# Splitting fp32 weights: the high part on GpSimd in one copy, every low part on VectorE

## The chip, the core and the metric

The kernel runs on one core of a Trainium2 chip, as one launch. The metric is device time in microseconds (us), from the start to the end of the execution. TensorE multiplies, VectorE (DVE) and ScalarE (ACT) do the elementwise work, GpSimd (POOL) helps with it, and SyncE (SP) issues most of the transfers from HBM. SBUF is the memory on the core that all of them read.

## The reference, cut to what matters

Two residual stacks of two layers run on 256 latent tokens (and, in the first stack, on 256 context tokens too), all in float32 with 1024 channels.

```
for l in range(2):                               # first stack
    context:  mixer (l = 0) or its memory only (l = 1), then FFN
    latent:   x = post(x, mixer(modulate(x)), gate);  x = post(x, ffn(modulate(x)), gate)
mixer = w_out( g_att * (attention @ w_att_o) + g_gla * (gated linear attention @ w_gla_o)
             + g_conv * (depthwise conv of 31 taps, layernorm, silu) @ w_conv_o )
for l in range(2):                               # second stack
    x += mix4(rmsnorm(x) @ w_in) @ w_o ;  x += (silu(h @ w_gate) * (h @ w_up)) @ w_down
```

Nearly all weights are used once per pass, as dense products of 256 tokens with matrices of 1024 or 2816 columns (the FFN is `silu(h @ gate) * (h @ up)` times `down`).

## The kernel before, in words

**The split.** A float32 product is made of three cheaper ones: a weight tile w is split into w_hi (w rounded to fp32r) and w_lo = w - w_hi, the activations into h_hi and h_lo, and TensorE adds w_hi h_hi, w_hi h_lo and w_lo h_hi (`dense`, L484 to L486; `dense_together`, L497 on; `token_major`, L512 on). A tile is 128 x 128 and meets 256 tokens, so one tile costs three matmuls.

**The stream.** All these tiles lie in HBM in the order of their use, as 723 loads of 8 tiles (128 x 1024 floats, 512 KB each). Three slots in SBUF hold a load's raw form, its high and its low part (`w_raw`, `w_hi`, `w_lo`, L211 to L213). For every load four things happen in turn. SP issues the transfer when the low part of the load three places earlier is made (L434). The high part is made when the transfer has landed and when TensorE has begun the load two places earlier, so that it is done with the old tiles of the slot (semaphore `w_used`). The low part is made from `w_raw` and `w_hi`. TensorE waits for the low part at a load's first tile (L456), and increments `w_used` with the load's first matmul.

**Who splits, before.** ACT makes the high part in two pieces of 512 columns (`split_to`, L1062 to L1074). ACT is in order: it evacuates each finished PSUM bank (`arrived` and `moved`), and `split_to` is called at those places, two to three loads ahead of TensorE. The low part is made by one of two engines, by a static plan. POOL makes it in the FFNs in one piece of 1024 columns, and in four pieces of 256 in the first loads of each pass, in the pass that only makes the context's memory and in the mixers of the second stack (`low_parts`, L1032 to L1055). DVE makes it in the three whole mixers of the first stack (`lows`, L1617 to L1624, called from `evac`), in one instruction of 1024 columns. `mixer_at` and `ffn_at` record at which loads these stretches begin. No low part is made by DVE in an FFN or in the second stack.

**What DVE does else.** In the mixers of the first stack it computes the depthwise convolution as a chain of multiply-adds of 256 columns (`convolve`, L1750 to L1765, 30 taps for 8 chunks), which is cut into 24 pieces of 10 instructions and placed between the other steps, many of them in the attention (L2125). It computes the scans and the differences of the gated linear attention (`gla`), the softmax's maxima and normalisation (`attention`), and all low parts of activations (`both_parts`, L1699, `low_part`, L1658). In an FFN it multiplies gate and up (L1739), splits the product (L1700, L1701) and adds the residual (L1718, L1723). The FFN is a loop of two turns, 33 loads each (`feed_forward`), so the counts of semaphores in it depend on the turn (`Place.value`, L377, with the increments of one turn in `PER_HALF`, L54).

**How far ahead.** `evac` lets DVE make all low parts up to one or two loads past the one that holds the chunk it is about to wait for; `tile_at` (L474) says where each chunk ends in the stream.

The functions with their lines:

Of the kernel before, what the change touches and what calls it, by code (L numbers as in the profile page):

```python
# [28 lines left out]
P = 128  # L29
D = 1024  # L30
KC = D // P
# [22 lines left out]
PER_HALF = {"lin_done": 2 * HALF + KC, "lin_evac": 2 * HALF + KC, "lo_ready": 3 * HALF, "hi_ready": 6 * HALF,  # L54
# [4 lines left out]
PIECES = 4  # L59
# [138 lines left out]
def program(nc, stream, first_in, ada_in, xt_in, cvec_in, vec1_in, vec2_in, glr_in, a2_in, const1_in, const2_in, small2_in, mask_in, out):  # L198
# [5 lines left out]
    with ExitStack() as ctx:  # L204
# [236 lines left out]
        ffn_at = []  # L441
        mixer_at = []
# [3 lines left out]
        def _(pe):  # L446
# [25 lines left out]
            def done(mm):  # L472
                mm.then_inc(sems["lin_done"], 1)
                if at.turn is None:  # L474
                    tile_at[n.at("lin_done")] = max(at.tile, tile_at.get(n.at("lin_done") - 1, 0))
# [209 lines left out]
            def feed_forward():  # L685
                h0 = n.at("h_ready") - KC
                ffn_at.append(at.tile // TILES)
# [110 lines left out]
            for turn, (l, s) in enumerate(PASSES):  # L798
# [35 lines left out]
                    mixer_at.append(at.tile // TILES)  # L834
# [195 lines left out]
        @block.gpsimd  # L1030
        def _(pool):
            def low_parts(first, last, pieces):  # L1032

                def one(load, slot):
                    for q in range(pieces):
                        if q * 2 % pieces == 0:
                            pool.wait_ge(sems["hi_ready"], load * 2 + (1 if q * 2 < pieces and pieces > 1 else 2))
                        part = slice(q * TILES * P // pieces, (q + 1) * TILES * P // pieces)
                        ins = pool.tensor_tensor(w_lo[:, slot, part], w_raw[:, slot, part], w_hi[:, slot, part].bitcast(F32), ALU.subtract)  # L1039
                    ins.then_inc(sems["lo_ready"], 1)  # L1040
                if last - first >= SLOTS:
                    with pool.Fori(0, (last - first) // SLOTS) as i:
                        for s in range(SLOTS):
                            one(i * SLOTS + (first + s), (first + s) % SLOTS)
                for load in range(last - (last - first) % SLOTS, last):
                    one(load, load % SLOTS)
            assert len(ffn_at) == 5 and len(mixer_at) == 3
            low_parts(0, SLOTS, PIECES)
            for k, load in enumerate(ffn_at):
                if k < len(mixer_at):  # L1050

                    pool.wait_ge(sems["lo_ready"], load)
                low_parts(load, load + 6 * HALF, 1)
                following = [x + SLOTS if x in mixer_at else x for x in sorted(mixer_at + ffn_at) + [LOADS] if x > load][0]
                low_parts(load + 6 * HALF, following, PIECES)  # L1055

        @block.scalar
        def _(act):
# [3 lines left out]
            def split_to(load):  # L1062

                while at.split < load:
                    m = at.split
                    at.split += 1
                    slot, turn = m % SLOTS, m // SLOTS
                    add = 16 * (turn + 1)
                    act.wait_ge(landed[slot], add if at.turn is None else at.turn * (16 * HALF) + add)
                    if m - SLOTS >= at.tile_done // TILES:  # L1070

                        act.wait_ge(sems["w_used"], at.value("w_used", m - SLOTS + 1))
                    for part in (slice(0, TILES * P // 2), slice(TILES * P // 2, TILES * P)):
                        act.activation(w_hi[:, slot, part], w_raw[:, slot, part], ACT.Copy).then_inc(sems["hi_ready"], 1)  # L1074

            def arrived(tiles=KC):

                at.tile += tiles
                if tiles:
                    split_to((at.tile - 1) // TILES + SLOTS)  # L1080
# [312 lines left out]
            def first_modulated():  # L1393
# [6 lines left out]
                split_to(SLOTS)  # L1400
# [201 lines left out]
            split_to(LOADS)  # L1602
# [3 lines left out]
        def _(dve):  # L1606
# [107 lines left out]
            def residual(x, alpha, means, early=None):  # L1714

                for c in range(KC):
                    dve.wait_ge(sems["lin_evac"], evac() if at.turn is None else at.up("lin_evac"))
# [14 lines left out]
            def feed_forward(x, scaled):  # L1732
                a, _ = CONST1["alpha"]
                with dve.Fori(0, 2) as i:
                    at.enter(i, dve_step=2 * HALF + (KC - 2) * scaled)
                    for c in range(HALF):
                        dve.wait_ge(sems["lin_evac"], at.up("lin_evac", 2))
# [6 lines left out]
                    at.leave()  # L1744
                dve.wait_ge(sems["r_ready"], at.now("r_ready"))
# [205 lines left out]
            def gla_memory(l, s):  # L1951
                n.up("lin_evac", 4 + len(MEMORY_UNITS[:2]))
                scans()
                for u in MEMORY_UNITS[2:]:
# [504 lines left out]
```

## Time and profile before

| | |
|---|---|
| median of 3 runs (lowest to highest) | 3263.15 us (3260.86 to 3266.92) |
| the profiled execution's own time | 3261.29 us |
| its span in the profile | 3259.5 us |
| mean granted TensorE clock | 0.94 |
| PE, PEld busy | 2966.9, 2806.7 us |
| DVE busy | 2195.1 us |
| ACT busy | 1517.4 us |
| POOL busy | 1057.0 us |

The table is one execution. Busy time is the time in which an engine had an instruction in work; it includes time in which an instruction had started and could not go on. PE is the matmul side of TensorE, PEld its weight loads. The span is cut below into stretches by their place in the kernel: the first mixer of the first stack runs from about 60 to 600 us, its FFN to about 840 us; the two other whole mixers begin near 860 and 1760 us, the pass that makes only the context's memory lies between 1660 and 1760 us, and the second stack begins near 2550 us.

### The profile page before, as it was taken

To read this page: it belongs to the slowest core of one execution; us is meant where nothing else is said; L and a number is where in the kernel's file an instruction comes from. 1 tells how busy PE (TensorE), PEld (TensorE's weight loads), DVE (VectorE), ACT (ScalarE), POOL (GpSimd) and SP (SyncE) were. 2 spreads that over 40 slices of the span, in tenths; PEclk is the share of its full clock that TensorE was granted. 3 is DMA by queue.
4 is the path that set the end of the run, shared out by engine and by line. 5 is a ranking of instruction groups with operands and counts; after the bars stand their busy time and mean duration, and the time that the engine had idled before them with its cause. 6 is when DMAs were issued, how large, how long until landed. Compare 5 with 4: busy or idle time off the path is not lost.

```text
span 3259.5 us, 57687 instructions
## 1 busy us (share of the span) xinstructions
PE 2966.9 (91%) x21812; PEld 2806.7 (86%) x21812; DVE 2195.1 (67%) x3303; ACT 1517.4 (47%) x3128; POOL 1057.0 (32%) x646
## 2 busy tenths in 40 slices
PE   8999979899889988989988899889899989998998
PEld 7998868899889878889978898679899869996998
DVE  6774787576778577775745775877666557646665
ACT  3544335444554424444454544235444454555554
POOL 1000000188200000037851000000388627873787
PEclk7999979899999988999989999889899989999999
DMA  6443324355444323435533443224455314541454
GB/s 240 150 154 111 123 90 146 105 183 175 135 155 137 103 97 102 145 109 171 181 98 110 150 152 101 77 73 154 153 175 180 105 53 161 172 155 56 144 176 164
DMA packets 120727, 441.85 MB, mean 136 GB/s; under 512 B 13456, under 2 KB 15504, under 8 KB 119872
## 3 DMA queue, kind: packets, MB, share of 16 engines
q1 hardware_dynamic: 108704, 393.35, 36.7%
q10 hardware_dynamic: 11808, 45.42, 4.1%
q8 instruction: 161, 2.64, 0.3%
q14 instruction: 54, 0.44, 0.0%
HBM read 437.67 MB, written 1.05 MB: 135 GB/s over the span
## 4 chain that ended last, share of the span: by engine, by line
PE 42%; issue 20%; DVE 17%; POOL 15%; ACT 5%; POOLq 0%; DMA 0%; SPq 0%; DVEq 0%; ACTq 0%
POOL w_lo L1039 15%; PE lin L484 9%; PE lin L486 9%; PE lin L485 9%; DVE arena L1763 7%; DVE w_lo L1622 3%; PE lin L534 3%; PE aux L734 2%; ACT w_hi L1074 1%; PE aux L597 1%; PE aux L622 1%; PE aux L588 1%; DVE small L1777 1%; ACT arena L1234 1%; DVE s_lo L1701 1%
## 5 line engine op out<-in xcount | busy, mean ns | idle before, releaser
L1039 POOL TENSOR_TENSOR w_lo<-w_raw,w_hi 128x1024 fp32r<-128x1024 f32 (+1 forms) x642 | 1056.8, 1666 | 2196.0 <-ACT w_hi L1074 2195.5
L484 PE MATMUL lin<-h_hi,w_hi 128*128 128x256 f32 x3584 | 1039.8, 290 | 47.0 <-DVE w_lo L1622 31.5
L485 PE MATMUL lin<-h_lo,w_hi 128*128 128x256 f32 x3584 | 1024.2, 286 | 0.0
L486 PE MATMUL lin<-h_hi,w_lo 128*128 128x256 f32 x3584 | 1023.5, 286 | 0.0
L1074 ACT ACTIVATE w_hi<-w_raw 128x512 fp32r<-128x512 f32 x1446 | 827.4, 623 | 119.2 <-PE lin L484 108.7
L484 PEld LDWEIGHTS lin<-h_hi,w_hi 128*128 128x128 f32 x3584 | 699.9, 195 | 59.4 <-issue 29.6
L485 PEld LDWEIGHTS lin<-h_lo,w_hi 128*128 128x128 f32 x3584 | 699.5, 195 | 0.4
L486 PEld LDWEIGHTS lin<-h_hi,w_lo 128*128 128x128 f32 x3584 | 698.0, 195 | 0.0
L1622 DVE TENSOR_TENSOR w_lo<-w_raw,w_hi 128x1024 fp32r<-128x1024 f32 x315 | 381.2, 1219 | 213.0 <-ACT w_hi L1074 211.7
L484 PE MATMUL lin<-s_hi,w_hi 128*128 128x256 f32 x1392 | 408.4, 293 | 16.6 <-DVE s_lo L1701 7.4
L485 PE MATMUL lin<-s_lo,w_hi 128*128 128x256 f32 x1392 | 400.9, 288 | 0.0
L486 PE MATMUL lin<-s_hi,w_lo 128*128 128x256 f32 x1392 | 400.6, 288 | 0.0
L484 PEld LDWEIGHTS lin<-s_hi,w_hi 128*128 128x128 f32 x1392 | 274.3, 197 | 24.7 <-issue 14.4
L1763 DVE SCALAR_TENSOR_TENSOR arena<-arena,vec 128x256 f32<-128x256 f32 x720 | 290.5, 477 | 0.0
L485 PEld LDWEIGHTS lin<-s_lo,w_hi 128*128 128x128 f32 x1392 | 274.8, 197 | 1.1 <-issue 0.8
L486 PEld LDWEIGHTS lin<-s_hi,w_lo 128*128 128x128 f32 x1392 | 274.3, 197 | 0.0
L1739 DVE TENSOR_TENSOR y_buf<-gate_buf,y_buf 128x256 f32<-128x256 f32 x110 | 151.1, 1374 | 181.8 <-ACT y_buf L1207 181.8
L1701 DVE TENSOR_TENSOR s_lo<-y_buf,s_hi 128x256 fp32r<-128x256 f32 x110 | 224.2, 2038 | 3.8
L534 PEld LDWEIGHTS lin<-cvec,a_raw 128*128 128x128 f32 x1280 | 165.1, 207 | 11.9 <-DMA a_raw<-in_ada 9.3
L534 PE MATMUL lin<-cvec,a_raw 128*128 128x2 f32 x1280 | 162.1, 257 | 7.9 <-DMA a_raw<-in_ada 7.9
L1640 DVE RECIPROCAL rstd<-std 128x256 f32<-128x256 f32 (+1 forms) x34 | 59.5, 1749 | 150.8 <-ACT std L1103 150.7
L1718 DVE SCALAR_TENSOR_TENSOR X<-X,gate_buf 128x256 f32<-128x256 f32 x72 | 75.5, 1049 | 125.0 <-ACT gate_buf L1215 67.1
(265 smaller groups left out, 4272.6 us busy)
## 6 DMA issues: line engine op xcount, KB each, us to landing
w_raw<-in_stream SPq DMA_DIRECT2D x723, 512.0 KB, 3.4
a_raw<-in_ada ACTq DMA_DIRECT2D x80, 512.0 KB, 3.4
arena<-in_first SPq DMA_DIRECT2D x2, 2048.0 KB, 19.6
X<-in_tokens SPq DMA_DIRECT2D x2, 1024.0 KB, 14.7
s_f<-in_ada SPq DMA_DIRECT2D x4, 512.0 KB, 10.5
arena<-in_ada SPq DMA_DIRECT2D x4, 512.0 KB, 17.3
arena<-in_const ACTq DMA_DIRECT2D x1, 1856.0 KB, 8.6
arena<-in_small ACTq DMA_DIRECT2D x1, 1536.0 KB, 12.7
```

The source lines that it names most:

```text
L484: used(pe.matmul(o, whi, hi[:, k, :], start=k == 0, stop=False), first)
L485: pe.matmul(o, whi, lo[:, k, :], start=False, stop=False)
L486: mm = pe.matmul(o, wlo, hi[:, k, :], start=False, stop=k == kcs - 1)
L534: mm = pe.matmul(o[:, 0:2], w[:, k, :], cvec[:, k, :], start=k == 0, stop=k == KC - 1)
L734: mm = pe.matmul(pair[kt][:, h * P:(h + 1) * P], part, part, start=True, stop=True)
L1039: ins = pool.tensor_tensor(w_lo[:, slot, part], w_raw[:, slot, part], w_hi[:, slot, part].bitcast(F32), ALU.subtract)
L1074: act.activation(w_hi[:, slot, part], w_raw[:, slot, part], ACT.Copy).then_inc(sems["hi_ready"], 1)
L1622: dve.tensor_tensor(w_lo[:, m % SLOTS, :], w_raw[:, m % SLOTS, :], w_hi[:, m % SLOTS, :].bitcast(F32), ALU.subtract).then_inc(sems["lo_rea ...
L1701: dve.tensor_tensor(lo, y, hi.bitcast(F32), ALU.subtract).then_inc(sems[name], 1)
L1718: dve.scalar_tensor_tensor(x[:, c, :], x[:, c, :], alpha, gate_buf[:, c % 2, :], ALU.mult, ALU.add).then_inc(sems["r_ready"], 1)
L1739: step(dve.tensor_tensor(y, gate_buf[:, c % 2, :], y, ALU.mult))
L1763: dve.scalar_tensor_tensor(CV[:, c, :], YP[:, c, tap:tap + S], v1(l, "conv_w", c * TAPS + tap), CV[:, c, :], ALU.mult, ALU.add).then_inc(s ...
```

## The change

The high part of every load is made by POOL in one `tensor_copy` of 1024 columns, as soon as the load has landed and `w_used` allows. The low part of every load is made by DVE (`lows`), in the FFN loops, the memory pass and the second stack too. ACT has neither. The static plan (`mixer_at`, `ffn_at`), `low_parts` and `split_to` are gone. `hi_ready` counts one per load where it counted two.

```
         def _(pool):
+            def high_part(s):
+                pool.tensor_copy(w_hi[:, s, :], w_raw[:, s, :]).then_inc(sems["hi_ready"], 1)
+            for load in range(USED + 2):
+                pool.wait_ge(landed[load % SLOTS], 16 * (load // SLOTS + 1))
+                if load >= SLOTS:
+                    pool.wait_ge(sems["w_used"], load + 1 - SLOTS)
+                high_part(load % SLOTS)
...
         def _(act):
-            def split_to(load):
...
             def moved(ins):
                 ins.then_inc(sems["lin_evac"], 1)
-                split_to(at.tile // TILES + SLOTS)
...
         def _(dve):
-            low_next = [0, 0]
+            low_next = [0]
             def lows(load):
-                first, last = low_next
-                for m in range(first, min(load, last)):
-                    dve.wait_ge(sems["hi_ready"], 2 * m + 2)
+                for m in range(low_next[0], load):
+                    dve.wait_ge(sems["hi_ready"], at.value("hi_ready", m + 1))
                     dve.tensor_tensor(w_lo[:, m % SLOTS, :], w_raw[:, m % SLOTS, :], w_hi[:, m % SLOTS, :].bitcast(F32), ALU.subtract
                                       ).then_inc(sems["lo_ready"], 1)
-                low_next[0] = max(first, min(load, last))
+                low_next[0] = max(low_next[0], load)
+            def lows_for(k):
+                lows(tile_at[n.at("lin_evac") + k] // TILES + SLOTS - 1)
             def evac(k=1):
-                c = n.up("lin_evac", k)
-                lows(tile_at[c] // TILES + SLOTS - 1)
-                return c
+                lows_for(k)
+                return at.up("lin_evac", k)
...
             def feed_forward(x, scaled):
                     for c in range(HALF):
-                        dve.wait_ge(sems["lin_evac"], at.up("lin_evac", 2))
+                        dve.wait_ge(sems["lin_evac"], evac(2))
```

`residual` in the FFN calls `evac` in the same way. In the memory pass the scans now carry the low parts between them. At the start two low parts stand before the first modulation (`lows(SLOTS - 1)`). In the second stack the waits for evacuations become `evac` calls, and `lows_for(8)` and `lows_for(2)` stand ahead of the first reciprocal and inside the pooling. POOL makes 720 high parts, so the last three loads of the padded stream are not split.

## Rows read from the trace of the kernel before

**Rows 1.** The page: busy time of each engine.

```profile
PE 2966.9 (91%) x21812; PEld 2806.7 (86%) x21812; DVE 2195.1 (67%) x3303; ACT 1517.4 (47%) x3128; POOL 1057.0 (32%) x646
```

**Rows 2.** Windows; the mixer's stretches and one in an FFN (busy us, count).

```profile
core 0: us, PE busy (x) PEld busy (x) DVE busy (x) ACT busy (x) POOL busy (x), PEclk, DMA share, GB/s
60.00:160.00 100.00, 93.08 (x743) 91.16 (x742) 74.29 (x129) 55.29 (x105) 0.00 (x0) 0.98 0.45 143
380.00:460.00 80.00, 64.00 (x444) 59.80 (x442) 75.84 (x185) 22.61 (x68) 0.00 (x0) 0.85 0.33 106
650.00:740.00 90.00, 88.24 (x734) 87.84 (x733) 63.79 (x47) 44.56 (x89) 76.87 (x32) 1.00 0.57 183
...
200.00:260.00 60.00, 59.87 (x506) 59.87 (x507) 52.22 (x74) 27.14 (x49) 0.00 (x0) 0.97 0.46 150
520.00:540.00 20.00, 13.44 (x96) 13.09 (x96) 19.35 (x43) 9.80 (x22) 0.00 (x0) 0.91 0.34 106
```

**Rows 3.** Windows of DVE's low parts alone (L1622), in mixer stretches of three passes.

```profile
60.00:160.00 100.00, 33.60 (x28) 0.98 0.45 143
380.00:460.00 80.00, 10.36 (x9) 0.85 0.33 106
...
200.00:260.00 60.00, 12.18 (x10) 0.97 0.46 150
520.00:540.00 20.00, 5.88 (x6) 0.91 0.34 106
...
1180.00:1260.00 80.00, 9.73 (x8) 0.88 0.33 111
...
2080.00:2190.00 110.00, 13.39 (x11) 0.84 0.23 72
```

**Rows 4.** The chain that ended last, by line, within 380 to 460 us.

```profile
by line: DVE arena L1763 67.3%; DVE w_lo L1622 10.0%; ACT arena L1234 6.2%; DVE small L1777 4.6%; DVE a_lo L1803 2.1%; DVE arena L1756 1.6%; ACT a_hi L1248 1.4%; DVE small L1782 1.3%; ACT w_hi L1074 1.3%; DVE M L1839 1.0%; DVE arena L1795 0
```

**Rows 5.** Groups of instructions with their shapes (busy us, mean ns, idle before).

```profile
L1039 POOL TENSOR_TENSOR w_lo<-w_raw,w_hi 128x1024 fp32r<-128x1024 f32 x330 | 808.1, 2453 | 1966.2 <-ACT w_hi L1074 1966.0
L1039 POOL TENSOR_TENSOR w_lo<-w_raw,w_hi 128x256 fp32r<-128x256 f32 x312 | 248.9, 834 | 229.8 <-ACT w_hi L1074 229.5
...
L1622 DVE TENSOR_TENSOR w_lo<-w_raw,w_hi 128x1024 fp32r<-128x1024 f32 x315 | 381.2, 1219 | 213.0 <-ACT w_hi L1074 211.7
L1763 DVE SCALAR_TENSOR_TENSOR arena<-arena,vec 128x256 f32<-128x256 f32 x720 | 290.5, 477 | 0.0
...
L1337 ACT ACTIVATE arena<-arena 128x1024 f32<-128x1024 f32 x48 | 50.6, 1053 | 22.7 <-DVE arena L1902 12.6 <-DVE arena L1897 6.6 <-issue 3.5
```

**Rows 6.** DVE's low parts of activations (L1701): duration min/median/max in ns.

```profile
L1701 DVE TENSOR_TENSOR s_lo<-y_buf,s_hi x110: 424/2511/2562, 652.3 to 3210.9; 128x256 fp32r<-128x256 f32 x110
L1701 DVE TENSOR_TENSOR s_lo<-s_f,s_hi x24: 424/426/427, 332.2 to 2031.0; 128x256 fp32r<-128x256 f32 x24
```

**Rows 7.** Timeline in an FFN, DVE and POOL from 699 us (start, us).

```profile
700.30 0.29 DVE L1700 CAST s_hi<-y_buf 128x256 fp32r<-128x256 f32 x1
700.63 2.51 DVE L1701 TENSOR_TENSOR s_lo<-y_buf,s_hi 128x256 fp32r<-128x256 f32 x1
...
700.38 2.48 POOL L1039 TENSOR_TENSOR w_lo<-w_raw,w_hi 128x1024 fp32r<-128x1024 f32 x1 [0.39 <-ACT w_hi L1074]
```

**Rows 8.** What PE waited for (us in total, times, longest).

```profile
PE lin L484 <- DVE w_lo L1622: 31.5, 19, 7.3
...
PE lin L484 <- POOL w_lo L1039: 12.6, 17, 1.0
PE lin L512 <- DVE w_lo L1622: 11.9, 9, 3.5
...
PE lin L512 <- POOL w_lo L1039: 9.0, 5, 4.0
...
PE lin L484 <- DVE s_lo L1701: 7.4, 10, 0.8
```

**Rows 9.** The page: the chain that ended last, by line.

```profile
POOL w_lo L1039 15%; PE lin L484 9%; PE lin L486 9%; PE lin L485 9%; DVE arena L1763 7%; DVE w_lo L1622 3%; PE lin L534 3%; PE aux L734 2%; ACT w_hi L1074 1%; PE aux L597 1%; PE aux L622 1%; PE aux L588 1%; DVE small L1777 1%; ACT arena L1234 1%; DVE s_lo L1701 1%
```

**Rows 10.** The second stack's pooling steps, DVE, from 2880 to 3030 us.

```profile
L2205 DVE TENSOR_TENSOR arena<-arena 128x542 f32<-128x542 f32 (+3 forms) x4 | 4.6, 1159 | 0.1
```

More of the change, by code:

```diff
@@ L52 @@
 NEG = -1e30
-PER_HALF = {"lin_done": 2 * HALF + KC, "lin_evac": 2 * HALF + KC, "lo_ready": 3 * HALF, "hi_ready": 6 * HALF,
+PER_HALF = {"lin_done": 2 * HALF + KC, "lin_evac": 2 * HALF + KC, "lo_ready": 3 * HALF, "hi_ready": 3 * HALF,
             "w_used": 3 * HALF, "s_ready": HALF, "r_ready": KC, "dve_step": 2 * HALF, "sum_ready": 1}
@@ L58 @@
 SLOTS = 3
-PIECES = 4
 ADA_CHUNKS = 6 * D // P
@@ L473, in done @@
                 mm.then_inc(sems["lin_done"], 1)
-                if at.turn is None:
-                    tile_at[n.at("lin_done")] = max(at.tile, tile_at.get(n.at("lin_done") - 1, 0))
+                tile_at[n.at("lin_done")] = max(at.tile, tile_at.get(n.at("lin_done") - 1, 0))
             def dense(hi, lo, ready=None, kcs=KC):
@@ L1031, in _ @@
         def _(pool):
[L1032 to L1055, printed above, removed]
+            def high_part(s):
[5 more added lines that the diff above has]
+                high_part(load % SLOTS)
         @block.scalar
@@ L1060, in _ @@
             n = at.n
-            def split_to(load):
[L1064 to L1074, printed above, removed]
             def arrived(tiles=KC):
                 at.tile += tiles
-                if tiles:
-                    split_to((at.tile - 1) // TILES + SLOTS)
                 act.wait_ge(sems["lin_done"], at.up("lin_done"))
@@ L1601, in _ @@
             at.tile_done = LOADS * TILES
-            split_to(LOADS)
         @block.vector
@@ L1716, in residual @@
                 for c in range(KC):
-                    dve.wait_ge(sems["lin_evac"], evac() if at.turn is None else at.up("lin_evac"))
+                    dve.wait_ge(sems["lin_evac"], evac())
                     dve.scalar_tensor_tensor(x[:, c, :], x[:, c, :], alpha, gate_buf[:, c % 2, :], ALU.mult, ALU.add
@@ L1744, in feed_forward @@
                     at.leave()
+                    assert low_next[0] == low_first + 3 * HALF
+                    low_next[0] += 3 * HALF
                 dve.wait_ge(sems["r_ready"], at.now("r_ready"))
@@ L1951, in gla_memory @@
             def gla_memory(l, s):
-                n.up("lin_evac", 4 + len(MEMORY_UNITS[:2]))
-                scans()
-                for u in MEMORY_UNITS[2:]:
-                    unit(l, u)
+                evac(4 + len(MEMORY_UNITS[:2]))
+                scans(lambda c: unit(l, MEMORY_UNITS[2:][c]))
                 dve.wait_ge(sems["x_ready"], n.at("x_ready"))
@@ L1997, in first_modulated @@
                 dve.tensor_tensor(wglr_lo[:, :], wglr[:, :], wglr_hi[:, :].bitcast(F32), ALU.subtract).then_inc(sems["glr_split"], 1)
+                lows(SLOTS - 1)
                 n.up("lin_evac", len(FIRST_UNITS) + len(FIRST_GROUPS))
@@ L2045, in _ @@
                         centre(before, early)
+                        evac(KVH + QT + 1)
                         scaled(early, lambda c: v1(pl, "ln2_g", c))
                         n.up("x_ready", KC)
-                        n.up("lin_evac", KVH + QT + 1)
                         inverse(aux[0], ROWS, name="row_ready")
+                        evac(2)
                         heads_normed(heads, {})
-                        n.up("lin_evac", 2)
                         gla_memory(l, s)
@@ L2057, in _ @@
                     y0, pieces = n.at("y_ready"), iter(range(CONV_PIECES))
-                    turns = [k for k, p in enumerate(PASSES) if whole(*p)]
-                    low_next[:] = mixer_at[turns.index(turn)] + SLOTS, ffn_at[turns.index(turn)]
                     for c in range(KC):
-                        if c == 0:
-                            dve.wait_ge(sems["lo_ready"], low_next[0])
                         dve.wait_ge(sems["lin_evac"], evac(2))
@@ L2189, in _ @@
                 step(dve.memset(w2["up"][:, :, 0:16], 0.0))
+                lows_for(8)
                 inverse(aux[0], slot=0)
@@ L2198, in _ @@
                 n.up("qk_normed")
-                dve.wait_ge(sems["lin_evac"], at.up("lin_evac", 9))
+                dve.wait_ge(sems["lin_evac"], evac(9))
                 prev, e = w2["up"], 16 + S
@@ L2206, in _ @@
                     prev = cur
+                lows_for(2)
                 ic = c2("inv_count").rearrange("p (c t) -> p c t", c=2)
@@ L2213, in _ @@
                 n.up("pooled_ready")
-                dve.wait_ge(sems["lin_evac"], at.up("lin_evac", 4))
+                dve.wait_ge(sems["lin_evac"], evac(4))
                 step(dve.tensor_tensor(w2["zp"][:, :, 2:], w2["gc"][:, :, :], w2["uc"][:, :, :], ALU.mult))
@@ L2225, in _ @@
                 cos, sin = c2("cos"), c2("sin")
-                dve.wait_ge(sems["lin_evac"], at.up("lin_evac", 3 + 2 * MH + 2))
+                dve.wait_ge(sems["lin_evac"], evac(3 + 2 * MH + 2))
                 dve.wait_ge(sems["rot_done"], at.up("rot_done"))
```

6 lines of the change are left out of this document (1 added, 5 removed).

## The prediction

> **What bounds the kernel now.** I began with the busy shares [rows 1]: PE is at 91% of the span, DVE at 67%, ACT at 47%, POOL at 32%. Those are averages over stages with different limits, so I cut the span into stretches [rows 2].
>
> In an FFN (650 to 740 us) PE is busy 88.24 of 90 us for 734 matmuls, 0.120 us each, or 24 x 0.120 = 2.89 us per load. There is nothing to win there but single waits. The chain puts 15% of the span on POOL's low parts [rows 9], but these lie beside a PE that is full; PE waited for them 12.6 + 9.0 us in the whole kernel [rows 8]. In the first stack's attention (380 to 460 us) it is the other way round: DVE 75.8 of 80 us, PE 64 with a granted clock of 0.85, and the chain in that stretch is DVE's convolution, 67.3%, and its low parts, 10.0% [rows 4]. Two shorter stretches are like it or near it: 520 to 540 us (DVE 19.35 of 20 us, PE 13.4) and 200 to 260 us (DVE 52.2 of 60, PE full) [rows 2]. So what the change is worth is read from DVE's time in the three whole mixers. In all of them POOL stands still today (0 us).
>
> **DVE and POOL get in each other's way.** This row decides the case. In FFNs the activation's low part, 256 columns, has a median of 2511 ns; the same instruction where POOL rests takes 426 ns [rows 6]. The timeline shows how: POOL starts at 700.38 and ends at 702.86, DVE's subtraction starts at 700.63 and ends at 703.14, 0.28 us after POOL [rows 7]. DVE waited for the whole of POOL's instruction, and only its fixed start of about 0.43 - 0.28 = 0.15 us was hidden. The cast at 700.30, with one input, ran its 0.29 us while POOL was starting. DVE's subtractions and convolution taps have two inputs in SBUF, and are of the kind that waited.
>
> **What moves.** ACT loses 1446 pieces, POOL its low parts. DVE gets 720 - 315 = 405 low parts more at 1.219 us [rows 5], 494 us of work. POOL gets 720 copies of 1024 columns. The queues of SP are not touched but for who releases them: the transfer of a load follows the low part, now always DVE's.
>
> **What one copy costs.** No row shows a one-input instruction of POOL. From below: a whole 1024-column instruction of ACT takes 1.053 us [rows 5], and I don't expect POOL to beat it. From above: the two-input one of the same size, 2.453 us. Between them, POOL's own slope: (2453 - 834) / 768 = 2.11 ns a column and 0.29 us fixed [rows 5]; if one input costs half of two, that is 0.29 + 1024 x 1.054 ns = 1.37 us, or 1.23 us if the fixed part halves too. I take 1.3 us, since the rows nearest to it are POOL's own. It adds 1.3 - 0.15 = 1.15 us to a DVE that has no idle time.
>
> The page "GPSIMD Engine Reference" of the Trainium skill (section 4.1, Engine selection) says that one-input work on GpSimd runs at roughly line rate, against about twice the time for two inputs. With one column per cycle of 1.2 GHz that would be an estimated 0.85 us and the fixed part, some 1.15 us, and the sum below would be about 22 us smaller. The page "SBUF — State Buffer" (section "SBUF: two separate sides") says that any GpSimd instruction that reads SBUF excludes DVE instructions with two SBUF inputs for its whole length. By that rule the copy blocks as the subtraction did; no row here shows it for a copy.
>
> **Losses, step by step.**
> - Attention: 9, 8 and 11 low parts fall in the DVE-bound stretches of the three passes [rows 3], so as many copies: 28 x 1.15 = 32 us. DVE is the chain there, so all of it counts.
> - Start of the mixer (60 to 160 us): DVE 74.29 + 28 x 1.15 = 106.5 us in 100 [rows 2, 3]: 6.5 us over, three passes, 20 us.
> - Linear attention (200 to 260 us): 52.22 + 10 x 1.15 = 63.7 in 60: 3.7 x 3 = 11 us.
> - Merge (520 to 540 us): 19.35 + 6 x 1.15 = 26.3 in 20; DVE has idle time right behind it, so I count half: 3 x 3 = 9 us.
> - Start of the kernel: two low parts ahead of the first modulation, 2 x 1.22 = 2.4 us.
> Together 74 us.
>
> **What is hidden.** FFN, two loads and one product: DVE 2 x 1.22 + 0.42 + 0.29 + 0.43 = 3.58 us, POOL 2 x 1.3 = 2.6 us. Even if they never overlap this is 6.18 us, less the hidden starts (five of 0.15) 5.4 us, against PE's 5.78 us. They are also out of step by nature: a copy follows the start of a load, the low part follows the copy. So the FFN costs nothing at 1.3 us; the cover is gone above about 1.5 us. Queued behind DVE's new waits for `hi_ready` are the FFN's products. The last low part asked for ahead of a product needs PE at the start of the load just before that product's end, 1.3 + 1.2 = 2.5 us of 2.89, so the product is not held. Second stack: the four pooling steps, 4.6 us [rows 10], stand between low parts, and two loads in hand cover 5.8 us. Zero, and if the cover breaks a few us per layer.
>
> **Gains.** POOL's low parts were late for PE by 12.6 + 9.0 us [rows 8], mostly where it takes four pieces of 0.834 us for a load that PE eats in 2.89 us; DVE's 1.22 us removes this. The FFN's last activation low part, blocked by POOL, cost 7.4 us at ten places, which goes too [rows 8]. ACT's high parts stand on the chain with 1% [rows 9], some 30 us; a copy of the same length takes their place, and only what came from ACT being busy elsewhere goes: 5 us. Together 34 us. What is late next is DVE's low part in the mixers (31.5 + 11.9 us of PE's waits already [rows 8]).
>
> **The sum** against the profiled execution: 3261.3 + 74 - 34 = 3301 us. That execution is 1.9 us below the median, so I say 3303 us, slower by 1.2%. A measurement of this kernel tells about 0.2% (6.5 us) from no change.
>
> **The rivals.**
> 1. *The copy is slow.* If POOL needs 1.7 us, a third of the way from my value to the upper bound, each copy costs 1.55: attention 43, mixer start (74.3 + 43.4 - 100) x 3 = 53, linear attention (52.2 + 15.5 - 60) x 3 = 23, merge 8.7 x 3 = 26, start 2; and the FFN is over by 3.58 + 3.4 - 0.75 - 5.78 = 0.45 us for each of 165 pairs, 74 us: 3261 + 221 - 34 = 3448 us. At the upper bound, 2.453 us, the same sum gives 267 us in the mixers and 1.95 x 165 = 322 in the FFNs: about 3816 us. For: POOL's other instruction is slow for its size. Against: it reads two inputs. Chance 0.19.
> 2. *The other side: ACT's queue was the hidden limit.* DVE stood idle 211.7 us before its low parts, waiting for ACT's high part [rows 5]. ACT is in order and makes it behind evacuations; POOL has nothing else and copies at once. If a good part of that idle time was ACT's and not PE's, DVE makes its low parts earlier and the collisions fall into time it had to spare. Then the stretches outside the attention cost nothing, attention pays at the lower bound, 28 x 0.9 = 25 us, and half of the 1% (33 us) that ACT's high parts have on the chain [rows 9] is gained: 3261 + 25 - 34 - 16 = 3236 us. It decides where ACT's lateness, not `w_used`, held the high part. Against: most of that idle lies where PE is full and where nobody is in a hurry. Chance 0.22.
> 3. *A wash.* The copy at the lower bound, 1.05 us: attention 25, linear attention 4, merge 7, start 2, mixer start none; 38 - 34 = +4 us: 3265 us. Chance 0.09.
> The forecast, a copy of 1.1 to 1.5 us that blocks DVE, keeps 0.5; its own range is 3275 to 3345 us.
>
> **Range and chances.** Down to 3230 us I take in rival 2, up to 3430 us the copies to about 1.65 us. Left out are the rest of rival 1 and what lies beyond rival 2, some 0.2. Faster 0.22, same 0.09, slower 0.69.
>
> **What would show it.** POOL's group has one form of 1024 columns with 1.2 to 1.4 us; 1.7 or more means rival 1. The convolution's taps, 477 ns before [rows 5], get a mean some 50 ns higher, with single ones near 1.6 us. PE's waits for DVE's low parts grow from 43 us, those for POOL vanish. The stretches of the three mixers become longer, attention most; the FFNs stay at 0.120 us per matmul. I am wrong if the taps keep their time, if the mixers become shorter, or if the FFN slows down while the copy is short.

## The result, and the profile after

| | before | after |
|---|---|---|
| median, measured together (lowest to highest) | 3265.03 us (3260.86 to 3267.48) | 3348.94 us (3346.33 to 3357.11) |
| the profiled execution's own time, span | 3261.29, 3259.5 us | 3351.34, 3349.5 us |

The ratio is 1.026 (95% interval 1.024 to 1.0285): slower by 2.6%, where 1.2% was forecast. The time lies inside the range (3230 to 3430 us) and the direction is the forecast's; the loss is twice the size. The page of after, its busy times and its chain by line (these answer to [rows 1] and [rows 9]):

```profile
PE 3008.8 (90%) x21812; PEld 2833.6 (85%) x21812; DVE 2440.8 (73%) x3708; ACT 768.4 (23%) x1682; POOL 894.0 (27%) x724
...
PE lin L480 14%; PE lin L481 13%; PE lin L482 13%; DVE arena L1727 8%; DVE w_lo L1580 6%; PE lin L530 3%; PE aux L729 3%; PE aux L593 2%; DVE rstd L1601 2%; POOL w_hi L1028 2%; DVE arena L1616 1%; PE aux L584 1%; ACT arena L1195 1%; DVE small L1741 1%; PE lin L493 1%
```

POOL's 15% of the chain are gone, and ACT's busy time is halved, yet DVE's convolution and low parts stand on the chain with 8% and 6% where they had 7% and 3%. PE's busy time grew by 41.9 us for the same 21812 matmuls, at a mean granted clock of 0.934 against 0.94: nearly half of the loss is not idle time in front of a matmul but PE taking longer over the same work. The groups of after with their shapes (busy us, mean ns, idle before; they answer to [rows 5]):

```profile
L1580 DVE TENSOR_TENSOR w_lo<-w_raw,w_hi 128x1024 fp32r<-128x1024 f32 x720 | 904.9, 1266 | 415.7 <-POOL w_hi L1028 409.4 <-DVE mod L1794 0.7
L1028 POOL CAST w_hi<-w_raw 128x1024 fp32r<-128x1024 f32 x720 | 893.8, 1243 | 2439.6 <-PE lin L480 1932.6 <-PE lin L493 314.3 <-DMA w_raw<-in_stream 127.3
...
L1727 DVE SCALAR_TENSOR_TENSOR arena<-arena,vec 128x256 f32<-128x256 f32 x720 | 334.2, 535 | 0.0
...
L1662 DVE TENSOR_TENSOR s_lo<-y_buf,s_hi 128x256 fp32r<-128x256 f32 x110 | 54.4, 495 | 3.8
```

The copy takes 1243 ns in the mean, the taps went from 477 to 535 ns, and the FFN's activation low part from a median of 2511 ns [rows 6] to a mean of 495 ns. The duration of the copies (min/median/max in ns):

```profile
L1028 POOL CAST w_hi<-w_raw x720: 1032/1096/5237, 33.1 to 3332.2; 128x1024 fp32r<-128x1024 f32 x180
```

So undisturbed it takes 1.03 to 1.1 us, and the mean is raised by copies that were themselves held up, one for 5.2 us. What PE waited for (us in total, times, longest), against [rows 8]:

```profile
PE lin L480 <- DVE w_lo L1580: 73.5, 49, 8.3
PE aux L646 <- DVE arena L1759: 63.4, 31, 5.5
PE aux L729 <- DVE arena L1876: 20.1, 21, 2.1
PE lin L508 <- DVE w_lo L1580: 16.2, 10, 3.8
```

DVE's low parts were late by 89.7 us instead of 43.4; POOL's 21.6 us are gone. (By 59.8 us they are late in e3, below, which has no copy on POOL: a third of the growth comes from moving the low parts alone.) New is the third line, products of the gated linear attention that wait for DVE's decays (L1876): 2.8 us in 4 waits in the trace of before.

**Where the 90 us lie.** Both kernels have the same 21812 matmuls in the same order, so the time between the same two matmuls can be compared stage by stage. The table does it for all traces of this study, as the difference to before in us (the three mixers summed, the five FFNs summed; the rows add up to what lies between the first and the last matmul). The experiments are those of the next section. A stage's value is one execution's. In e4, whose edit touches the second stack alone, the linear attention still moves by 5.5 us against after, so a difference of that size between two columns shows nothing by itself.

| stage (us in before) | after | e1 | e2 | e3 | e4 | e5 | e6 | e7 | e8 |
|---|---|---|---|---|---|---|---|---|---|
| start, mixer's first part (414) | +11.4 | +31.5 | +27.5 | -1.3 | +11.8 | +12.1 | -1.7 | +1.5 | +12.6 |
| gated linear attention (305) | +27.5 | +1.9 | +1.1 | -0.1 | +22.0 | +24.7 | +0.9 | +3.9 | -1.5 |
| q and k heads (289) | +11.6 | +11.9 | +14.6 | -1.6 | +12.5 | +9.5 | -1.4 | -1.5 | +3.8 |
| attention (337) | +17.3 | +8.8 | +19.3 | +1.1 | +17.6 | +18.6 | +1.0 | +1.0 | +7.7 |
| merge to next norm (464) | +19.1 | +26.1 | +34.9 | -4.9 | +19.6 | +15.1 | -2.6 | -6.6 | +11.8 |
| FFNs (994) | -4.8 | -7.6 | -0.6 | -18.9 | -4.4 | -7.8 | -21.2 | -2.8 | -0.7 |
| memory pass (109) | -10.1 | -4.3 | +0.1 | -2.4 | -8.9 | -9.0 | -5.2 | -1.5 | -0.3 |
| second stack's mixers (323) | +20.6 | +10.7 | +3.2 | +5.3 | +15.0 | +11.4 | +4.5 | +23.5 | +0.2 |

In after the three mixers lose 86.9 us, FFNs and memory pass win 14.9, and the second stack, which the prediction had at zero, loses 20.6.

**A gain inside the first row.** Its +11.4 us are a loss of 28.0 and a gain of 16.6. The gain lies in the stretch from the first of the mixer's four token-major products (`token_major`, two loads each) to the first product of the linear attention (38 us per pass in before): 5.4, 5.5 and 5.7 us shorter in the three passes. e4 and e5 have it too (17.0 and 16.0), e3 has not (0.3). In before, and below it in after:

```profile
142.68 1.23 DVE L1868 SCALAR_TENSOR_TENSOR arena<-arena 128x1024 f32<-128x1024 f32 x1 [5.83 <-ACT arena L1329]
144.55 1.20 DVE L1622 TENSOR_TENSOR w_lo<-w_raw,w_hi 128x1024 fp32r<-128x1024 f32 x1
145.89 0.55 PE L512 MATMUL lin<-w_hi,h_hi 128*128 128x256 f32 x1 [3.48 <-DVE w_lo L1622]
...
150.29 1.45 DVE L1832 SCALAR_TENSOR_TENSOR arena<-arena 128x1024 f32<-128x1024 f32 x1 [3.12 <-ACT arena L1290]
153.73 0.36 PE L508 MATMUL lin<-w_hi,h_hi 128*128 128x256 f32 x1 [1.51 <-DVE w_lo L1580]
```

DVE waits in order for a result of ACT, with the next low part behind it, and PE waits for that. Without the high parts ACT delivers sooner: PE waits 1.51 us instead of 3.48, and the clock granted in the four products is 1.00 instead of 0.94.

### The profile page after: what moved, and what is told of

It reads as the page before. It is cut to its first block, busy times and chain, and to the rows that moved or that the text cites. A ratio compares the mean times of both kernels' runs of the same rounds, so it can differ in the third digit from the quotient of the medians.

```text
span 3349.5 us, 56812 instructions
## 1 busy us (share of the span) xinstructions
PE 3008.8 (90%) x21812; PEld 2833.6 (85%) x21812; DVE 2440.8 (73%) x3708; ACT 768.4 (23%) x1682; POOL 894.0 (27%) x724
## 3 DMA queue, kind: packets, MB, share of 16 engines
HBM read 437.67 MB, written 1.05 MB: 131 GB/s over the span
## 4 chain that ended last, share of the span: by engine, by line
PE 59%; DVE 30%; ACT 4%; issue 3%; POOL 2%; DMA 2%; SPq 0%; DVEq 0%; ACTq 0%; POOLq 0%
PE lin L480 14%; PE lin L481 13%; PE lin L482 13%; DVE arena L1727 8%; DVE w_lo L1580 6%; PE lin L530 3%; PE aux L729 3%; PE aux L593 2%; DVE rstd L1601 2%; POOL w_hi L1028 2%; DVE arena L1616 1%; PE aux L584 1%; ACT arena L1195 1%; DVE small L1741 1%; PE lin L493 1%
## 5 line engine op out<-in xcount | busy, mean ns | idle before, releaser
L1028 POOL CAST w_hi<-w_raw 128x1024 fp32r<-128x1024 f32 x720 | 893.8, 1243 | 2439.6 <-PE lin L480 1932.6
L1580 DVE TENSOR_TENSOR w_lo<-w_raw,w_hi 128x1024 fp32r<-128x1024 f32 x720 | 904.9, 1266 | 415.7 <-POOL w_hi L1028 409.4
L480 PE MATMUL lin<-h_hi,w_hi 128*128 128x256 f32 x3584 | 1055.7, 295 | 76.7 <-DVE w_lo L1580 67.1
L481 PE MATMUL lin<-h_lo,w_hi 128*128 128x256 f32 x3584 | 1037.0, 289 | 0.0
L481 PEld LDWEIGHTS lin<-h_lo,w_hi 128*128 128x128 f32 x3584 | 712.1, 199 | 0.4
L1727 DVE SCALAR_TENSOR_TENSOR arena<-arena,vec 128x256 f32<-128x256 f32 x720 | 334.2, 535 | 0.0
L530 PEld LDWEIGHTS lin<-cvec,a_raw 128*128 128x128 f32 x1280 | 164.1, 206 | 12.8 <-DMA a_raw<-in_ada 10.6
L530 PE MATMUL lin<-cvec,a_raw 128*128 128x2 f32 x1280 | 161.2, 257 | 9.0 <-DMA a_raw<-in_ada 9.0
L1701 DVE TENSOR_TENSOR y_buf<-gate_buf,y_buf 128x256 f32<-128x256 f32 x110 | 115.1, 1047 | 45.9 <-ACT y_buf L1168 44.7
L646 PEld LDWEIGHTS aux<-const,arena 128*128 128x128 f32 x224 | 30.9, 170 | 95.2 <-DVE arena L1759 90.6
L508 PE MATMUL lin<-w_hi,h_hi 128*128 128x256 f32 x320 | 94.3, 295 | 17.1 <-DVE w_lo L1580 16.2
L729 PE MATMUL aux<-arena 128*128 128x128 f32 x672 | 89.9, 290 | 20.3 <-DVE arena L1876 20.1
## 6 DMA issues: line engine op xcount, KB each, us to landing
s_f<-in_ada SPq DMA_DIRECT2D x4, 512.0 KB, 10.1
arena<-in_small ACTq DMA_DIRECT2D x1, 1536.0 KB, 10.8
```

Source lines behind the costliest of these rows:

```text
L480: used(pe.matmul(o, whi, hi[:, k, :], start=k == 0, stop=False), first)
L481: pe.matmul(o, whi, lo[:, k, :], start=False, stop=False)
L508: mm = pe.matmul(o[:, 0:2 * P], xhi, whi, start=k == 0, stop=False)
L530: mm = pe.matmul(o[:, 0:2], w[:, k, :], cvec[:, k, :], start=k == 0, stop=k == KC - 1)
L729: mm = pe.matmul(pair[kt][:, h * P:(h + 1) * P], part, part, start=True, stop=True)
L1028: pool.tensor_copy(w_hi[:, s, :], w_raw[:, s, :]).then_inc(sems["hi_ready"], 1)
```

## The experiments

The timing runs of e1 to e4 stand beside before at 3263.01 us, those of e5 to e8 at 3263.24 us.

**e1: the copy released earlier.** In after, POOL waits for `w_used`, which PE increments with the first matmul of the next load. ACT had started right behind the evacuation of the chunk that ends the old load. e1 gives POOL the end of that chunk (`lin_done`) as its release, outside the FFNs. That is ACT's release where a chunk is one load. In the token-major products a chunk spans two loads; there ACT waited for `w_used`, as after's POOL does, and e1 holds the first load's copy until the second load's products are done.

```
-                if load >= SLOTS:
-                    pool.wait_ge(sems["w_used"], load + 1 - SLOTS)
+                old = load - SLOTS
...
+                    pool.wait_ge(sems["lin_done"], min(c for c, tile in tile_at.items() if tile >= TILES * (old + 1)))
```

> The changed kernel, but outside the FFNs POOL waits for the matmul that ends the old load of the slot (lin_done of its chunk) in place of w_used, which comes with the first matmul of the next load. Theory A, late release: in the linear attention an ada unit and a gram stand between two loads, so w_used comes 2 to 4 us late, DVE stands in order before the low part, and its decay for the next gram behind it. Then the three linear-attention stretches, +27.5 us in the changed kernel, fall to +5 to +12, and the time goes from 3349 to 3322 to 3335 us. Theory B, the lock alone: the copies are as many and as long, so nothing changes by more than 5 us, 3344 to 3354 us.

Measured: 3338.14 us (3336.85 to 3340.71), ratio 1.0234 (1.0217 to 1.0251), between the two expected ranges. The gated linear attention falls from +27.5 to +1.9 us. The cycle that does it, in the timeline of after (start, us):

```profile
220.84 1.04 POOL L1028 CAST w_hi<-w_raw 128x1024 fp32r<-128x1024 f32 x1 [5.41 <-PE lin L480]
221.91 1.23 DVE L1580 TENSOR_TENSOR w_lo<-w_raw,w_hi 128x1024 fp32r<-128x1024 f32 x1 [1.55 <-POOL w_hi L1028]
223.06 0.69 DVE L1875 TENSOR_TENSOR arena<-arena 128x512 f32<-128x512 f32 x1
223.66 0.69 DVE L1876 TENSOR_TENSOR arena<-arena 128x512 f32<-128x512 f32 x1
...
223.29 1.84 PE L530 MATMUL lin<-cvec,a_raw 128*128 128x2 f32 x16
225.00 2.03 PE L729 MATMUL aux<-arena 128*128 128x128 f32 x16
226.78 0.36 PE L480 MATMUL lin<-h_hi,w_hi 128*128 128x256 f32 x1
...
227.28 1.04 POOL L1028 CAST w_hi<-w_raw 128x1024 fp32r<-128x1024 f32 x1 [5.40 <-PE lin L480]
228.36 1.23 DVE L1580 TENSOR_TENSOR w_lo<-w_raw,w_hi 128x1024 fp32r<-128x1024 f32 x1 [1.55 <-POOL w_hi L1028]
229.50 1.22 DVE L1815 TENSOR_TENSOR s_f<-arena 128x1024 f32<-128x1024 f32 x1
230.63 0.68 DVE L1875 TENSOR_TENSOR arena<-arena 128x512 f32<-128x512 f32 x1
231.24 0.69 DVE L1876 TENSOR_TENSOR arena<-arena 128x512 f32<-128x512 f32 x1
...
231.98 3.65 PE L729 MATMUL aux<-arena 128*128 128x128 f32 x16 [2.08 <-DVE arena L1876]
```

PE is done with the old load at 223.3 us. Between it and the next load stand a unit of the modulation (L530) and the products of the linear attention (L729), and only then, at 226.78 us, comes the matmul that counts `w_used`. DVE is in order: it stands idle for 1.55 us before the low part, the decays (L1875, L1876) of the next products are queued behind it, and where another 1.22 us instruction joins the queue (229.50) PE waits 2.08 us. In before, ACT started 0.28 us after the evacuation's start:

```profile
219.62 0.39 ACT L1292 ACTIVATE M<-lin 128x256 f32<-128x256 f32 x1 [3.32 <-PE lin L486]
219.90 1.14 ACT L1074 ACTIVATE w_hi<-w_raw 128x512 fp32r<-128x512 f32 x2
221.08 1.23 DVE L1622 TENSOR_TENSOR w_lo<-w_raw,w_hi 128x1024 fp32r<-128x1024 f32 x1 [0.99 <-ACT w_hi L1074]
```

DVE idles 0.99 us there. In e1 PE's waits for those decays are down from 20.1 us in 21 waits to 3 (its waits, as above):

```profile
PE aux L731 <- DVE arena L1882: 1.7, 3, 0.8
```

The late release is shown as the cause in this stage. As it stands the edit is no remedy, though: the mixer's first part and the merge lose 27 us more than in after. Of these, 12.2 us lie in the stretch of the token-major products, where the edit releases one copy of two later. A copy of after there (from 159.96) and two of e1 (from 161.40):

```profile
159.96 1.49 POOL L1028 CAST w_hi<-w_raw 128x1024 fp32r<-128x1024 f32 x1 [1.21 <-PE lin L508]
...
161.40 2.03 POOL L1030 CAST w_hi<-w_raw 128x1024 fp32r<-128x1024 f32 x2 [4.41 <-PE lin L512]
```

For the rest the cause is open. The net gain is 10.8 us; a release that keeps `w_used` in the token-major products was not run.

**e2: the lock alone.** To the kernel before, which splits in the old way, POOL adds one useless copy of 1024 columns per load of the three whole mixers, from a constant into a spare buffer, released by `w_used`. Nobody waits for it but the next copy.

```
+                    pool.wait_ge(sems["w_used"], load + 1 - SLOTS)
+                    pool.tensor_copy(spare[:, 0:1024], const1[:, 0:1024]).then_inc(sems["spared"], 1)
```

> The kernel before, with nothing moved; in the three whole mixers POOL makes one further copy of 1024 columns per load, from a constant to a spare buffer that nobody reads, gated on w_used. It has the lock of the change and none of its waits. If the lock is all of the mixers' loss (+87 us over the stretches), the time goes from 3265 to 3335 to 3350 us, with +7 to +10 us in each linear-attention stretch. If the late release is what costs there, the linear attention loses under 4 us per pass, and the whole is 3295 to 3320 us.

Measured: 3362.97 us (3361.23 to 3370.04), ratio 1.0316 (1.0299 to 1.0333). 315 copies that no result depends on cost 100 us, more than either range expected. The groups of e2:

```profile
L1060 POOL CAST spare<-const 128x1024 bf16<-128x1024 f32 x315 | 422.4, 1341 | 1328.3 <-PE lin L485 1206.8 <-PE lin L513 76.5 <-PE lin L498 44.7
L1776 DVE SCALAR_TENSOR_TENSOR arena<-arena,vec 128x256 f32<-128x256 f32 x720 | 338.9, 542 | 0.0
```

The taps are stretched as in after (542 against 535 ns). The loss lies in the same stages as after's, except the linear attention, which loses 1.1 us: the 27.5 us there are not the lock. In after all eleven copies between 200 and 290 us took 1.04 us, so none met DVE. In e2 copies do meet it in this stage, and 25 of DVE's instructions run 21.0 us longer together, yet only 1.1 us are paid. Two things differ from after's copies: these write bf16, and no low part follows each of them, so it is an upper measure of the lock rather than its exact share.

**e3: no copy on GpSimd at all.** After's kernel, all low parts on DVE, but the high parts made by ACT as before (`split_to` is back); POOL does nothing.

```
-                high_part(load % SLOTS)
...
+                split_to(at.tile // TILES + SLOTS)
```

> The changed kernel with the high part back on ACT as before (two pieces, split_to at the evacuations) and POOL with nothing to do: the move of the low parts alone. Theory A and B both take the mixers back to within 3 us of before per pass. What is left is the low parts' move: the memory pass 8 to 12 us shorter, the FFNs 3 to 8 us shorter together, the second stack's mixers 12 to 18 us longer: 3258 to 3270 us. If the second stack's loss came from the copies too, 3245 to 3256 us.

Measured: **3237.26 us** (3235.76 to 3238.84), ratio 0.9925 (0.9908 to 0.9941), faster than both kernels and below both expected ranges. The low parts' move was worth more than I thought: 18.9 us in the FFNs, where 3 to 8 were expected. Its busy times and taps:

```profile
PE 2959.9 (92%) x21812; PEld 2805.1 (87%) x21812; DVE 2165.4 (67%) x3708; ACT 1513.7 (47%) x3124; POOL 0.2 (0%) x4
...
L1739 DVE SCALAR_TENSOR_TENSOR arena<-arena,vec 128x256 f32<-128x256 f32 x720 | 290.6, 477 | 0.0
```

DVE executes the 3708 instructions of after in 2165.4 instead of 2440.8 us: 275 us of after's busy DVE were no work. In before it needed 2195.1 us for 3303 instructions [rows 1]: 407 of them ran over 0.1 us longer than the same kind does in e3, by 509 us together, 460 of them in the FFNs. They are not only those with two inputs. The cast of one input was held too, up to 2535 ns in before against 293:

```profile
L1700 DVE CAST s_hi<-y_buf x110: 293/295/2535, 649.9 to 3210.6; 128x256 fp32r<-128x256 f32 x110
```

So the two halves of the change part here: low parts on DVE are worth 26 us, and the high parts on POOL cost 3348.94 - 3237.26 = 112 us. PE's busy time is 3008.8 us in after and 2959.9 in e3, so 49 of the 112 us are PE taking longer over the same matmuls. Part of that is its clock: after spends 441 us at the lower of the two granted levels (1.2 GHz) and e3 386 us, which is worth at most half of the difference, an estimated 27 us.

**e4: the second stack's order.** After's DVE makes no low part while it computes two reciprocal square roots in turn. The timeline of after:

```profile
2650.42 1.22 DVE L1580 TENSOR_TENSOR w_lo<-w_raw,w_hi 128x1024 fp32r<-128x1024 f32 x1 [1.65 <-POOL w_hi L1028]
2653.28 1.75 DVE L1601 RECIPROCAL rstd<-std 128x256 f32<-128x256 f32 x1 [1.65 <-ACT std L1064]
...
2658.13 1.75 DVE L1601 RECIPROCAL rstd<-std 128x256 f32<-128x256 f32 x1
...
2661.70 1.22 DVE L1580 TENSOR_TENSOR w_lo<-w_raw,w_hi 128x1024 fp32r<-128x1024 f32 x1
```

Ten us pass from the end of one low part to the start of the next, where PE eats a load in 2.89 us; PE waits 4.1 us for it. e4 puts low parts between the two (one line, `lows_for(10)`, ahead of the second).

> The changed kernel with two low parts moved ahead in DVE's order in the second stack: between the two chains of reciprocals, where DVE makes no low part for 8.4 us and PE waits 4.1 us. If this order is the loss (+8.5 and +7.4 us in the two mixers of the second stack), some 3 to 5 us per layer come back: 3339 to 3344 us. If the copies are what delays the low parts there, under 1 us per layer: 3347 to 3350 us.

Measured: 3345.94 us (3342.72 to 3353.54), ratio 1.0263 (1.0246 to 1.028), no difference to after that can be told. The mixers of the second stack go from +20.6 to +15.0 us, no more than the linear attention moves, which the edit doesn't touch. So what the order costs is not shown; e3, which has the same order, loses 5.3 us there, and more than that it can't be.

**e5: the copy in two pieces.** After's copy as two of 512 columns.

```
+                for part in (slice(0, TILES * P // 2), slice(TILES * P // 2, TILES * P)):
+                    ins = pool.tensor_copy(w_hi[:, s, part], w_raw[:, s, part])
```

> The changed kernel with POOL's copy in two pieces of 512 columns. If DVE loses the length of one POOL instruction per collision, a shorter one lets DVE in between: the taps' mean falls from 535 towards 505 ns, and the time by 5 to 20 us, 3328 to 3344. If what counts is POOL's whole time per load, two fixed parts make it longer (by 0.15 to 0.3 us per load), and with it hi_ready later: 3350 to 3365 us.

Measured: 3335.77 us (3333.39 to 3337.36), ratio 1.0223 (1.0206 to 1.024); 13 us less than after. The groups of e5:

```profile
L1029 POOL CAST w_hi<-w_raw 128x512 fp32r<-128x512 f32 x1440 | 1074.1, 774 | 2241.5 <-PE lin L480 1772.7 <-PE lin L493 299.9 <-DMA w_raw<-in_stream 110.7
L1729 DVE SCALAR_TENSOR_TENSOR arena<-arena,vec 128x256 f32<-128x256 f32 x720 | 338.6, 541 | 0.0
```

POOL is busy longer (1074 against 894 us) and the taps are no shorter, so the time came inside the range of the first theory while its sign, taps towards 505 ns, did not. The largest part of the gain is the second stack's 9.2 us; those of merge and FFNs (4.0 and 3.0) are within what two traces differ by. Why shorter holds help there and not in the attention (+18.6 against +17.3) was not followed.

**e6: the best of both.** e3, with POOL used in the two stretches where before or after was better than e3: its copy of the high part for 13 loads of the memory pass, and the low parts in four pieces of 256 columns in the second stack's mixers, as before.

```
+            low_loads[:] = [m for a, f in zip(second_at, ffn_at[3:]) for m in range(a + 2, f)]
+            high_loads[:] = range(memory_at[0] + SLOTS, mixer_at[2])
```

> e3_act_high with two parts given to POOL where the trace says that they pay: the high parts of the memory pass (the changed kernel gained 10.1 us there, e3 2.4) and the low parts of the second stack's mixers in four pieces, as before (e3 loses 2.7 and 2.5 us there). If the stages add up, 3237 - 7.7 - 5 = 3224 us, 3219 to 3230. If the hand-overs between the engines cost as much as they give, 3232 to 3240 us.

Measured: **3230.54 us** (3227.06 to 3234.77), ratio 0.9896 (0.9878 to 0.9914), 1% faster than before and the fastest version of this study, 6.7 us below e3 and between the two ranges. The memory pass gains 5.2 us (e3: 2.4), the second stack loses 4.5 us (e3: 5.3); both differences are small beside what two traces differ by, so the traces don't show which part brought the gain. After's memory pass gained 10.1; where the rest of that went is open.

**e7: the lock in the rest of the kernel.** e3 with e2's spare copies everywhere except in the three whole mixers.

> e3_act_high with a spare POOL copy of 1024 columns per load in all stages except the first stack's three whole mixers; nothing waits for these copies. If the lock is why the changed kernel is slower than e3 in the FFNs (-5 against -19 us, five together) and in the second stack (+21 against +5 us), then here too the FFNs lose 10 to 16 us against e3 and the second stack 8 to 18: 3258 to 3272 us. If it was the later high part there (w_used in place of the evacuation), nothing waits for a copy here: 3237 to 3245 us.

Measured: 3271.7 us (3262.8 to 3277.22, 10 runs), ratio 1.0021 (1.0011 to 1.0031), so the 394 copies cost some 34 us against e3, inside the expected range. Its trace is of an execution of 3276.2 us, 4.5 us above the median. The FFNs go from -18.9 to -2.8 us and the second stack's mixers from +5.3 to +23.5, near after's -4.8 and +20.6. A collision in e7's FFN:

```profile
650.07 1.04 POOL L1042 CAST spare<-const 128x1024 bf16<-128x1024 f32 x1 [0.56 <-PE lin L482]
650.14 1.25 DVE L1690 TENSOR_TENSOR s_lo<-y_buf,s_hi 128x256 fp32r<-128x256 f32 x1
```

The 256-column subtraction takes 1.25 us where it takes 0.426 us in e3, and ends 0.28 us after the copy, the same distance as in [rows 7]. The lock is what took the FFN's gain back and what costs most in the second stack. In the FFNs PE waits for DVE's low parts 24 times in after (9.3 us) and 27 times in e7 (11.8 us), in e3 3 times (1.0 us). In the second stack PE's waits grow by only 3.5 of the 15.3 us between e3 and after; there the granted clock falls from 0.927 to 0.886, and in e7 to 0.892.

**e8: half the length.** e2 with 512 columns in place of 1024.

> e2_spare with copies of 512 columns instead of 1024: the same number, about half the length. If the mixers' loss (100 us at 1.34 us a copy) goes by POOL's time less some 0.15 us of hidden start, (0.8 - 0.15) / (1.34 - 0.15) = 0.55 of it stays: 3310 to 3328 us. If each collision costs a fixed amount however long the copy, it stays above 3340 us. If the loss comes only when DVE's backlog exceeds its slack, under 3300 us.

Measured: 3296.27 us (3294.89 to 3298.34), ratio 1.0102 (1.0085 to 1.0119). The groups of e8:

```profile
L1060 POOL CAST spare<-const 128x512 bf16<-128x512 f32 x315 | 299.2, 950 | 1388.4 <-PE lin L485 1258.1 <-PE lin L513 86.3 <-PE lin L498 43.7
L1776 DVE SCALAR_TENSOR_TENSOR arena<-arena,vec 128x256 f32<-128x256 f32 x720 | 313.5, 506 | 0.0
```

The same number of copies costs 33 us instead of 100, as the third theory expected. A copy's cost is not in proportion to its length. DVE's instructions in the whole mixers run some 159 us longer in e2 than in before, and 67 us in e8 (counted as above): where DVE has slack, only what exceeds it is paid. In the attention, where it has next to none, all is paid: 20.0 us of longer instructions and a stage 19.3 us longer in e2, 8.5 and 7.7 in e8.

## Why the prediction was half right

The direction and the mechanism were right; the sum was not. It had +40 us, as 74 of losses less 34 of gains; the traces have +92.6, as 115.4 (after minus e3) less 22.8 (e3 against before). By stage, beside the terms of the forecast, and with the time by which DVE's instructions run longer in after than in e3 (those over 0.1 us longer than the median of their kind in e3; 396 of them):

| | forecast | after - e3 | DVE held longer |
|---|---|---|---|
| start and mixer's first part, up to the token-major products | 22 | 28.9 | 38.1 |
| token-major products | 0 | -16.3 | 14.1 |
| gated linear attention | 11 | 27.6 | 0 |
| q and k heads | 0 | 13.2 | 21.6 |
| attention | 32 | 16.2 | 19.9 |
| merge | 9 | 24.0 | 45.6 |
| FFNs | 0 | 14.1 | 115.0 |
| second stack's mixers | 0 | 15.3 | 22.2 |
| memory pass | 0 | -7.7 | 5.2 |
| sum | 74 | 115.4 | 282 |

**The mechanism was right.** The copy excludes DVE's instructions with two inputs in SBUF, and its one-input casts too, as the subtraction did: taps rise by 58 ns (forecast: some 50), PE's waits for POOL vanish, and e2 shows that nothing but the exclusion is needed for the loss in the whole mixers outside the linear attention. The page "SBUF — State Buffer" of the Trainium skill (section "SBUF: two separate sides") calls it an exclusive lock for the whole instruction. The held instructions agree: DVE's end 0.28 us behind POOL's. The page also gives the lock to whoever starts first; by the starts in the trace that does not always hold, as the copy of 5.24 us below shows.

**The copy's length was right in the mean, its price was not.** 1.3 us was taken, 1.243 us is the mean. But the mean adds two things: 1.04 us undisturbed (just below my lower bound, ACT's 1.053 us) and the time for which the copy is held up itself, which DVE does not pay. What DVE paid for a meeting is 0.8 us (4.83 against 4.04 below, 1.25 against 0.43 in e7), where the sum took 1.15. That 1.3 met the mean is luck. The estimate from the page "GPSIMD Engine Reference", 1.15 us, was nearer to the undisturbed copy, and what the page says of one input agrees: the shortest copies are 607 ns for 512 columns (e5) and 1032 ns for 1024, 0.83 ns a column. Rival 1 is out, and so is rival 3, whose copy of 1.05 us was the undisturbed one: the length of the copy did not decide.

**The attention: "all of it counts" held, the price failed.** 28 x 1.15 = 32 us were forecast, 16.2 came. 33 copies fell into the stage and made 28 of DVE's instructions longer by 19.9 us, 0.71 us each; nearly all of that was paid. So the term that was mis-sized is the 1.15 us per copy. It let DVE lose more than it did where POOL came first, and it let POOL win every meeting. The timeline of after, from 411 us:

```profile
411.63 4.83 DVE L1727 SCALAR_TENSOR_TENSOR arena<-arena,vec 128x256 f32<-128x256 f32 x10
...
417.03 4.04 DVE L1727 SCALAR_TENSOR_TENSOR arena<-arena,vec 128x256 f32<-128x256 f32 x10
420.99 0.68 DVE L1741 TENSOR_REDUCE small<-aux 128x2 f32<-128x512 f32 x1
...
411.77 1.25 POOL L1028 CAST w_hi<-w_raw 128x1024 fp32r<-128x1024 f32 x1 [8.46 <-PE lin L480]
416.73 5.24 POOL L1028 CAST w_hi<-w_raw 128x1024 fp32r<-128x1024 f32 x1 [3.72 <-PE lin L480]
```

The first copy delays ten taps by 0.8 us (4.83 against 4.04): it gets in behind the first of them. The second delays them by nothing: it comes in only when DVE's run of back-to-back taps is over, at about 421 us, and ends at 421.97, 5.24 us after its start. DVE loses nothing, and the high part is late instead. Both copies start while DVE is in a run of taps; what decides between them is not shown. Such long holds are few: 20 of the 720 copies took over twice the shortest.

**The gated linear attention failed on a step that was not in the sum.** Its 11 us were collisions, and in after there were none (no DVE instruction of this stage was held). The 27.6 us come from the release: the text ahead of the prediction lets the high part wait for `w_used` in the kernel before, and the prediction says that "POOL has nothing else and copies at once". Neither read that ACT's copy was freed by the evacuation of the old load's last chunk, a modulation unit and a block of linear-attention products ahead of the next load's first matmul. e1 shows this.

**Merge, heads and the mixer's first part** were costed from single windows, and half of the merge's excess was waved away with the idle time behind it. 24.0 and 13.2 us came against 9 and 0, and 28.9 against 22 in the first part. The windows of before can't say which of DVE's instructions a copy will meet. e2 measures the lock in these stages at 27.5 (with the token-major products) + 14.6 + 34.9 us with longer copies.

**"So the FFN costs nothing" and "Zero" for the second stack failed.** They cost 14.1 + 15.3 = 29 us; with the heads' 13.2, terms put at nothing cost 43 us. The two were balances of busy time: 5.4 us of work in 5.78 for the FFN's two loads, two loads in hand for the second stack. That the totals fit did not keep every low part on time: 24 came late for PE in the FFNs, 3 in e3. The FFNs gained 18.9 us without the copies and 4.8 with them; the second stack loses 15.3 to the copies. With the late release in the linear attention (27.6 against 11) these are the steps that made the loss twice the forecast. The over-sized attention, and the gains in the next paragraphs, hid a part of the error.

**Not in the sum at all: PE's own time.** The losses were priced as DVE's excess alone, and a lower clock was put at nothing. After's PE is busy 49 us longer than e3's over the same matmuls, at a granted clock of 0.934 against 0.94.

**Gains.** 34 us were forecast for what POOL's late parts cost. e3 gets 26 us in all (22.8 between the traces), so the term was near, but in the FFNs most of it is to be had only while POOL stands still.

**Rival 2** is out as a whole, since the time rose, but its mechanism is there in two places. In the token-major products ACT's relief was worth 16.3 us (after against e3), and in the memory pass after is 7.7 us better than e3. The forecast had 5 us for ACT's relief.

## What to carry to other kernels

Before moving work to GpSimd beside a VectorE that is two thirds busy, measure the lock alone: one useless copy per step in the kernel as it is costs 100 us here, and it can be run before any line of the change is written. When a producer changes engine, compare what releases it in the order of PE's instructions and not only its duration: here the next load's first matmul, in place of the old load's last, cost some 26 us in one stage. Look for what the old engine does better once it is relieved, too: that was worth 16 us here. A balance of busy times over a period does not show that an in-order engine has the part ready in time.

## What the runs showed of the hardware

A GpSimd copy can be held through many DVE instructions and not only through one: 5.24 us for a copy of 1.04 us, until a run of ten back-to-back taps had ended, though another copy got in behind the first tap of such a run; 1.03 us was the shortest of 720 and 1.10 us the median. DVE's cast of one input is held as well as its subtraction of two: up to 2.54 us for 0.29. And 315 copies of 1024 columns cost 100 us where as many of 512 cost 33 us, though their mean durations are 1.341 and 0.950 us.
